# HGRN2 scan of a hybrid decoder: two of its mask levels computed by products of 64 keys and 32 queries

## The chip, the cores and the metric

The kernel runs on one core of a Trainium2 chip. The metric is the device time of one launch in microseconds, as the median over several runs. TensorE (PE in the profile) multiplies, VectorE (DVE) does elementwise work and reads the results, ScalarE (ACT) evaluates functions, GpSimd (POOL) splits weights into a high and a low part, and the SyncE queue (SP) loads the weights.

## The reference

Two decoder layers run on 512 prompt tokens and 8 groups of 4 sample tokens. Each layer is a half-step FFN, a mixer with three parallel recurrent branches (HGRN2, GLA, mLSTM) and a second half-step FFN. The change is in the first branch's scan, which computes:

```python
def gated_linear_scan(q, k, v, logf, s0):
    """S_t = diag(exp(logf_t)) S_{t-1} + k_t v_t^T ; o_t = S_t^T q_t, chunkwise and exactly per-token causal."""
    c = chunk_len(q.shape[2])
    tri = jnp.tril(jnp.ones((c, c), dtype=bool))

    def step(s, inp):
        qc, kc, vc, gc = inp
        b = jnp.cumsum(gc, axis=2)
        diff = b[:, :, :, None, :] - b[:, :, None, :, :]
        decay = jnp.exp(jnp.where(tri[:, :, None], diff, NEG_BIG))
        att = jnp.einsum('bhtd,bhsd,bhtsd->bhts', qc, kc, decay)
        o = (jnp.einsum('bhts,bhsv->bhtv', att, vc)
             + jnp.einsum('bhtd,bhdv->bhtv', qc * jnp.exp(b), s))
        ...
        return s_new, o
```

The scan has 4 heads with 128 features each. The matrix `att` holds, for a query t and a key s of one chunk, a product over the features in which each feature has a decay of its own.

## The kernel before

Activations lie with features on the 128 partitions and the 544 tokens along the free axis. Dense products (L723) run three times for each pair of operands: high by high, high by low, low by high. They take their weights from a stream that SP loads and POOL splits, and each is 128 x 128 weights by 272 tokens.

The kernel works on chunks of 128 tokens, so a head has four of them. The decay is a product over the tokens between key and query, so the kernel builds `att` in seven levels. Level l pairs blocks of 2^l tokens: the keys of a block's first half meet the queries of its second half. After each level, `qkt_update` multiplies decays into Q, K and T for the next level (L1949, L1952, L1956 on DVE), so that level l+1 can't be computed before level l has been read and updated.

A level is one step of the written-out order `ORDER`, of kind "lv". `weave` puts halves of dense tiles between the steps, one to four of them (`HALVES_BEHIND`), so that PE has work while DVE evaluates a step. PE's part of a step waits for `dve_step` and `act_step`, that is until both have done with the step before it. It increments `pe_step` with its last product. DVE's part waits for that and increments `dve_step` at its end (L2126).

In a level up to the fifth, PE computes for each head and chunk four products: 32 keys as the weights, by the 16 queries of these 32 tokens that lie in second halves (L915). The product of keys g to g+32 lands on partitions g to g+32 of PSUM tensor SA. That makes 4 x 4 x 4 = 64 products. Each product of 32-bit floats appears in the profile as two LDWEIGHTS and two MATMUL records, so a level has 128 MATMUL records. Levels 1 and 2 end with four products for the sample tokens (L835), eight records. The sixth and seventh level have one product for each block (L920): 32 keys by 32 queries, and 64 keys by 64 queries.

DVE reads SA with four COPY_PREDICATED instructions (L2015), one for each group of 32 partitions, under the level's mask of bytes. It writes only the 32 x 32 squares on the diagonal of `attC`.

The second branch (GLA, `br == 1`) uses the same code with two heads to a product. The scans follow one another in each of the two layers. In this profile the first branch's levels 1 to 7 begin on PE between 523 and 582 us in the first layer, and between 1924 and 1982 us in the second.

Of the kernel before, what the change touches and what calls it, by code (L numbers as in the profile page):

```python
# [32 lines left out]
HEADS, CH = 4, 128  # L33
NCH = SEQ // CH
# [205 lines left out]
def build(nc, wst, xT, par_d, lb_d, const_d, lvm_d, fg_d, st_h, st_g, st_c, st_n, st_m,  # L240
          yT, p_h, p_g, p_c, p_n, s_h, s_g, s_c, s_n, s_m, x_keep):
    ctx = ExitStack()
    with ctx:
# [110 lines left out]
        SA = ctx.enter_context(nc.psum_tensor("SA", [P, 2, 512], F32))  # L354
# [65 lines left out]
        half_of = const[:, C_DIAG + 100:C_DIAG + 102]  # L420
        pairs = const[0:SMP, C_DIAG + 104:C_DIAG + 108]
        colK = const[:, C_DIAG + 108:C_DIAG + 116]

        def mask(l):
            return lvm[:, (l - 1) * P:l * P]
# [7 lines left out]
        def kt(br, h):  # L433

            return h // 2 if br == 1 else h
# [271 lines left out]
        def _(pe):  # L707
# [153 lines left out]
            def step(L, s):  # L861
                kind, br, h = s
# [5 lines left out]
                mm = None  # L868
# [29 lines left out]
                elif kind == "d":  # L898
                    for i in range(2):
                        hh = 2 * h + i  # L900
# [4 lines left out]
                        mm = sample_products(br)  # L905
                elif kind == "lv":
                    bs, hf = 1 << h, 1 << (h - 1)
                    o = SA[:, 0, 0:HEADS * NCH * 16].rearrange("p (h c b) -> p h c b", h=HEADS, c=NCH)
                    n = 2 if br == 1 else 1
                    for hh in range(0, HEADS, n):  # L910
                        for c in range(NCH if hf < 32 else 0):
                            for g in range(4):
                                s0 = c * CH + 32 * g
                                q = Q[:, hh:hh + n, s0:s0 + 32].rearrange("p h (n b) -> p h n b", b=bs)[:, :, :, hf:bs]
                                mm = pe.matmul(o[32 * g:32 * g + 32, hh:hh + n, c, :].rearrange(  # L915
                                    "p h (n b) -> p h n b", b=hf), K[:, kt(br, hh), s0:s0 + 32], q, start=True, stop=True)
                        for c in range(NCH if hf >= 32 else 0):
                            for s0 in range(0, CH, bs):
                                o0 = c * 64 + s0 // bs * hf
                                mm = pe.matmul(SA[s0:s0 + hf, hh // 2, :].rearrange("p (h n) -> p h n", h=2)[  # L920
                                                   :, hh % 2:hh % 2 + n, o0:o0 + hf],
                                               K[:, kt(br, hh), c * CH + s0:c * CH + s0 + hf],
                                               Q[:, hh:hh + n, c * CH + s0 + hf:c * CH + s0 + bs],
                                               start=True, stop=True)
# [592 lines left out]
        def _(dve):  # L1517
# [446 lines left out]
            def step(L, s):  # L1964
# [40 lines left out]
                elif kind == "lv":  # L2005
                    dve.sem_inc(dve_began, 1)
                    bs, hf = 1 << h, 1 << (h - 1)
                    for s0 in range(0, CH if hf >= 32 else 0, bs):
                        n0 = s0 // bs * hf
                        a = attQ[s0:s0 + hf, :, :].rearrange("p h (c t) -> p h c t", t=CH)  # L2010
                        src = SA[s0:s0 + hf, :, :].rearrange("p a (b c t) -> p (a b) c t", b=2, c=NCH)
                        ch.did(dve.tensor_copy(a[:, :, :, s0 + hf:s0 + bs], src[:, :, :, n0:n0 + hf]))
                    for j in range(4 if hf < 32 else 0):
                        g = slice(32 * j, 32 * j + 32)
                        ch.did(dve.copy_predicated(  # L2015
                            attC[g, :, g].rearrange("p c (n b) -> p c n b", b=bs)[:, :, :, hf:bs],
                            mask(h)[g, g].rearrange("p (n b) -> p n b", b=bs)[:, :, hf:bs].unsqueeze(1).to_broadcast(
                                [32, HEADS * NCH, 32 // bs, hf]),
                            SA[g, 0, 0:HEADS * NCH * 16].rearrange("p (c n b) -> p c n b", c=HEADS * NCH, b=hf)))
                    if h <= S_LEVELS:  # L2020
                        ch.did(dve.copy_predicated(
                            attS,
# [328 lines left out]
```

## Time and profile before

| | |
|---|---|
| median of 3 runs | 2846.6 us (2843.3 to 2848.44) |
| the profiled execution | 2846.17 us, span 2844.4 us |
| PE busy | 2810.3 us, 99% of the span |
| DVE, ACT, POOL busy | 59%, 33%, 56% |
| TensorE clock granted, mean | 0.997 of full speed |
| share of PE in the chain that ended last | 93% |

A MATMUL record lasts longer than its place in the stream, since matmuls are pipelined. What a group of products costs PE is the distance from its first start to the start of the group behind it.

### The profile page before, as it was taken

What the parts mean: (1) busy time and instruction counts of PE and PEld (TensorE: products, weight loads), DVE (VectorE), ACT (ScalarE), POOL (GpSimd) and SP (SyncE); (2) the same over time, 40 slices, a digit from 0 to 9 for tenths busy, and PEclk for the clock granted to TensorE, in tenths of its full rate; (3) what the DMA queues carried; (4) which work ended last, traced back from release to release, by engine and by line L of the source; (5) the groups of instructions that cost most, each with busy time, mean ns of one, the idle gap of its engine ahead of it and who ended that gap; (6) DMA issues with size and microseconds to landing.
All of it is one profiled execution on the core that took longest, in us unless ns stands there. A gap on an engine that the chain in (4) does not pass through costs nothing.

```text
span 2844.4 us, 63198 instructions
## 1 busy us (share of the span) xinstructions
PE 2810.3 (99%) x24828; PEld 2766.3 (97%) x24828; DVE 1689.4 (59%) x2419; ACT 950.6 (33%) x1616; POOL 1596.5 (56%) x1466
## 2 busy tenths in 40 slices
PE   8999999999999999999999999999999999999998
PEld 7999999999999999999999999999999999999998
DVE  8554677545553578383784637766454446783645
ACT  4221233123152425151452414330412523452433
POOL 6666676556654674525464352766565556734343
PEclk9999999999999999999999999999999999999999
DMA  5796835665654655353444433355665557453532
GB/s 191 199 247 191 237 101 182 170 154 155 185 167 111 189 163 162 117 175 110 126 144 140 156 120 109 121 169 169 160 181 153 161 151 186 148 170 118 158 123 78
DMA packets 196956, 444.27 MB, mean 156 GB/s; under 512 B 13464, under 2 KB 57664, under 8 KB 195904
## 3 DMA queue, kind: packets, MB, share of 16 engines
q1 hardware_dynamic: 107360, 281.09, 30.4%
q0 software_dynamic: 40128, 125.83, 18.7%
q10 hardware_dynamic: 49248, 34.28, 4.0%
q8 instruction: 154, 2.52, 0.4%
q14 instruction: 66, 0.54, 0.1%
HBM read 422.64 MB, written 144.35 MB: 199 GB/s over the span
## 4 chain that ended last, share of the span: by engine, by line
PE 93%; DVE 3%; ACT 1%; POOL 1%; issue 1%; ACTq 0%; DVEq 0%; PEld 0%; POOLq 0%
PE dense L723 60%; PE SA L783 15%; PE SB L783 11%; POOL Wl L588 1%; PE SA L998 1%; PE SA L915 1%; PE SA L859 1%; PE SA L1001 1%; PE SA L903 1%; PE SA L846 0%; PE SA L920 0%; POOL Wh L586 0%; PE SB L1005 0%; PE SA L848 0%; PE SA L855 0%
## 5 line engine op out<-in xcount | busy, mean ns | idle before, releaser
L588 POOL TENSOR_TENSOR Wl<-raw,Wh 128x512 fp32r<-128x512 f32 x620 | 854.0, 1377 | 51.8
L586 POOL TENSOR_SCALAR Wh<-raw 128x512 fp32r<-128x512 f32 x620 | 450.9, 727 | 672.8 <-PEq L728 445.8
L723 PE MATMUL dense<-Hh,Wh 128*128 128x272 f32 x2768 | 585.8, 293 | 15.2 <-POOLq L590 10.1
L723 PE MATMUL dense<-Hh,Wl 128*128 128x272 f32 x2768 | 573.9, 289 | 0.5 <-issue 0.5
L723 PE MATMUL dense<-Hl,Wh 128*128 128x272 f32 x2768 | 572.6, 288 | 0.0
L723 PEld LDWEIGHTS dense<-Hh,Wh 128*128 128x128 f32 x2768 | 435.0, 189 | 25.7 <-issue 16.2
L723 PEld LDWEIGHTS dense<-Hl,Wh 128*128 128x128 f32 x2768 | 436.7, 189 | 0.0
L723 PEld LDWEIGHTS dense<-Hh,Wl 128*128 128x128 f32 x2768 | 434.0, 189 | 0.8 <-issue 0.8
L651 POOL TENSOR_TENSOR Sl<-pair,Sh 128x512 fp32r<-128x512 f32 x120 | 173.7, 1465 | 421.8 <-ACT Sh L1088 421.0
L723 PE MATMUL dense<-Ah,Wh 128*128 128x272 f32 x1408 | 291.9, 289 | 0.8 <-DVE X L1814 0.7
L723 PE MATMUL dense<-Al,Wh 128*128 128x272 f32 x1408 | 290.7, 288 | 0.0
L723 PE MATMUL dense<-Ah,Wl 128*128 128x272 f32 x1408 | 290.2, 287 | 0.0
L1814 DVE SCALAR_TENSOR_TENSOR X<-dense,X 128x544 f32 x64 | 46.3, 724 | 296.4 <-PE dense L723 295.9
L723 PEld LDWEIGHTS dense<-Ah,Wh 128*128 128x128 f32 x1408 | 220.6, 188 | 1.6 <-DVE X L1814 0.9
L723 PEld LDWEIGHTS dense<-Al,Wh 128*128 128x128 f32 x1408 | 221.3, 188 | 0.0
L723 PEld LDWEIGHTS dense<-Ah,Wl 128*128 128x128 f32 x1408 | 220.3, 189 | 0.0
L1088 ACT ACTIVATE Sh<-pair 128x512 fp32r<-128x512 f32 x240 | 143.9, 624 | 33.3 <-PE SA L783 33.2
L1088 ACT ACTIVATE Sh<-wsum 128x512 fp32r<-128x512 f32 x180 | 113.2, 630 | 100.0 <-PE SA L783 50.5
L1589 DVE TENSOR_TENSOR Sl<-wsum,Sh 128x512 fp32r<-128x512 f32 x180 | 136.3, 759 | 0.0
L1104 ACT ACTIVATE tmp<-SA 128x272 f32<-128x272 f32 x60 | 22.8, 381 | 269.1 <-PE SA L783 269.1
L1589 DVE TENSOR_TENSOR Sl<-pair,Sh 128x512 fp32r<-128x512 f32 x120 | 104.1, 867 | 12.4 <-ACT Sh L1088 12.4
L1681 DVE TENSOR_TENSOR Al<-tmp,Ah 128x544 f32 (+1 forms) x88 | 69.0, 784 | 40.9 <-ACT Ah L1130 20.9
(473 smaller groups left out, 6317.4 us busy)
## 6 DMA issues: line engine op xcount, KB each, us to landing
raw<-wst SPq DMA_DIRECT2D x276, 512.0 KB, 3.7
w_sums<-wst POOLq DMA_DIRECT2D x36, 1536.0 KB, 13.3
w_sums<-wst POOLq DMA_DIRECT2D x18, 2048.0 KB, 16.8
pair<-wst SPq DMA_DIRECT2D x120, 256.0 KB, 3.5
pair<-w_sums SPq DMA_DIRECT2D x60, 512.0 KB, 3.7
wsum<-w_sums SPq DMA_DIRECT2D x60, 512.0 KB, 3.6
w_sums<-w_sums POOLq DMA_DIRECT2D x12, 1536.0 KB, 9.0
wsum<-wst SPq DMA_DIRECT2D x60, 256.0 KB, 2.5
```

The source lines that it names most:

```text
L586: pool.tensor_scalar(Wh[:, j, cs], raw[:, j, cs], 1.0, 0.0, ALU.mult, ALU.add).then_inc(glink, 1)
L588: pool.tensor_tensor(Wl[:, j, cs], raw[:, j, cs], f32(Wh[:, j, cs]), ALU.subtract).then_inc(glink, 1)
L651: pool.tensor_tensor(Sl[:, q, :], slot(q), f32(Sh[:, q, :]), ALU.subtract).then_inc(q_lo_pool, 1)
L723: mm = pe.matmul(out[:, a, 0:HALF], w[:, ring, w0:w0 + 128], x[:, k, a * HALF:(a + 1) * HALF], start=(k == 0 and n == 0), stop=(k == nk - ...
L783: mm = pe.matmul(out, w[:, q, k * 128:(k + 1) * 128], xs[:, k, :], start=(opens and k == 0 and m == 0), stop=(k == 3 and m == 2), skip_gro ...
L859: return pe.transpose(out, in_, idn)
L903: mm = pe.matmul(SA[:, i, cs], K[:, kt(br, hh), cs], Q[:, hh, cs], start=True, stop=True)
L915: mm = pe.matmul(o[32 * g:32 * g + 32, hh:hh + n, c, :].rearrange("p h (n b) -> p h n b", b=hf), K[:, kt(br, hh), s0:s0 + 32], q, start=Tr ...
L1088: act.activation(Sh[:, q, :], slot(q), ACT.Copy).then_inc(q_hi, 1)
L1589: TT(Sl[:, q, :], slot(q), f32(Sh[:, q, :]), ALU.subtract).then_inc(q_lo, 1)
L1681: TT(Al[:, at, :], tmp[:, j:j + 1, :], f32(Ah[:, at, :]), ALU.subtract).then_inc(ffn_lo, 1)
L1814: STT(xs, dps[j % 2][:, :, 0:HALF], 0.5, xs, ALU.mult, ALU.add).then_inc(slot_free[j % 2], 1)
```

## The change

In the first branch alone, levels 2 and 4 take 64 keys and the 32 queries of these 64 tokens in one product. A level then has 4 x 4 x 2 = 32 products (64 MATMUL records) where it had 64 (128 records). A product lands on 64 partitions and 32 columns. Half of its result belongs to keys and queries of different groups of 32 and isn't read. The result of a level fills 512 columns of SA where it filled 256. DVE's four instructions stay in number, elements and destination. They read 16 columns out of each 32. Levels 1, 3, 5, 6 and 7, and the whole of the second branch, are as before.

```diff
--- before.py
+++ after.py
@@ -421,6 +421,10 @@
         pairs = const[0:SMP, C_DIAG + 104:C_DIAG + 108]
         colK = const[:, C_DIAG + 108:C_DIAG + 116]
 
+        def level_keys(br, l):
+
+            return 64 if br == 0 and l in (2, 4) else 32
+
         def mask(l):
             return lvm[:, (l - 1) * P:l * P]
 
@@ -905,15 +909,16 @@
                         mm = sample_products(br)
                 elif kind == "lv":
                     bs, hf = 1 << h, 1 << (h - 1)
-                    o = SA[:, 0, 0:HEADS * NCH * 16].rearrange("p (h c b) -> p h c b", h=HEADS, c=NCH)
+                    wide = level_keys(br, h)
+                    o = SA[:, 0, 0:HEADS * NCH * wide // 2].rearrange("p (h c b) -> p h c b", h=HEADS, c=NCH)
                     n = 2 if br == 1 else 1
                     for hh in range(0, HEADS, n):
                         for c in range(NCH if hf < 32 else 0):
-                            for g in range(4):
-                                s0 = c * CH + 32 * g
-                                q = Q[:, hh:hh + n, s0:s0 + 32].rearrange("p h (n b) -> p h n b", b=bs)[:, :, :, hf:bs]
-                                mm = pe.matmul(o[32 * g:32 * g + 32, hh:hh + n, c, :].rearrange(
-                                    "p h (n b) -> p h n b", b=hf), K[:, kt(br, hh), s0:s0 + 32], q, start=True, stop=True)
+                            for g in range(0, CH, wide):
+                                s0 = c * CH + g
+                                q = Q[:, hh:hh + n, s0:s0 + wide].rearrange("p h (n b) -> p h n b", b=bs)[:, :, :, hf:bs]
+                                mm = pe.matmul(o[g:g + wide, hh:hh + n, c, :].rearrange(
+                                    "p h (n b) -> p h n b", b=hf), K[:, kt(br, hh), s0:s0 + wide], q, start=True, stop=True)
                         for c in range(NCH if hf >= 32 else 0):
                             for s0 in range(0, CH, bs):
                                 o0 = c * 64 + s0 // bs * hf
@@ -2010,13 +2015,15 @@
                         a = attQ[s0:s0 + hf, :, :].rearrange("p h (c t) -> p h c t", t=CH)
                         src = SA[s0:s0 + hf, :, :].rearrange("p a (b c t) -> p (a b) c t", b=2, c=NCH)
                         ch.did(dve.tensor_copy(a[:, :, :, s0 + hf:s0 + bs], src[:, :, :, n0:n0 + hf]))
+                    wide = level_keys(br, h)
                     for j in range(4 if hf < 32 else 0):
                         g = slice(32 * j, 32 * j + 32)
                         ch.did(dve.copy_predicated(
                             attC[g, :, g].rearrange("p c (n b) -> p c n b", b=bs)[:, :, :, hf:bs],
                             mask(h)[g, g].rearrange("p (n b) -> p n b", b=bs)[:, :, hf:bs].unsqueeze(1).to_broadcast(
                                 [32, HEADS * NCH, 32 // bs, hf]),
-                            SA[g, 0, 0:HEADS * NCH * 16].rearrange("p (c n b) -> p c n b", c=HEADS * NCH, b=hf)))
+                            SA[g, 0, 0:HEADS * NCH * wide // 2].rearrange("p (c e t) -> p c e t", c=HEADS * NCH, t=16)[
+                                :, :, j % (wide // 32), :].rearrange("p c (n b) -> p c n b", b=hf)))
                     if h <= S_LEVELS:
                         ch.did(dve.copy_predicated(
                             attS,
```

## Rows read from the trace of the kernel before

**Rows 1.** The page, engine busy times, clock by slices and chain that ended last

```profile
PE 2810.3 (99%) x24828; PEld 2766.3 (97%) x24828; DVE 1689.4 (59%) x2419; ACT 950.6 (33%) x1616; POOL 1596.5 (56%) x1466
...
PE 93%; DVE 3%; ACT 1%; POOL 1%; issue 1%; ACTq 0%; DVEq 0%; PEld 0%; POOLq 0%
```

**Rows 2.** Waits of PE over the span: who waited for whom, total us, times, longest

```profile
PE SA L915 <- issue: 2.2, 2, 1.7
PE SA L915 <- DVEq L2126: 1.4, 4, 0.5
```

**Rows 3.** Timeline of PE, level 1, first layer: start, us, record, idle before

```profile
523.25 1.24 PE L915 MATMUL SA<-setA,kbuf 128*32 128x16 f32 x126
...
524.36 0.39 PE L835 MATMUL SB<-setA,kbuf 128*32 128x32 f32 x7
524.67 0.52 PE L723 MATMUL dense<-Hh,Wh 128*128 128x272 f32 x2
```

**Rows 4.** Timeline of PE, level 4, first layer

```profile
555.86 1.26 PE L915 MATMUL SA<-setA,kbuf 128*32 128x16 f32 x128 [0.50 <-DVEq L2126]
557.05 0.52 PE L723 MATMUL dense<-Hh,Wh 128*128 128x272 f32 x2
```

**Rows 5.** Timeline of PE, levels 6 and 7, first layer

```profile
574.04 1.21 PE L920 MATMUL SA<-setA,kbuf 128*32 128x32 f32 x64
575.18 0.40 PE L723 MATMUL dense<-Hh,Wh 128*128 128x272 f32 x1
...
581.40 2.08 PE L920 MATMUL SA<-setA,kbuf 128*64 128x64 f32 x32
583.41 0.40 PE L723 MATMUL dense<-Hh,Wh 128*128 128x272 f32 x1
```

**Rows 6.** Timeline of PE, third branch, second layer: products of 64 weight columns

```profile
2297.38 0.63 PE L965 MATMUL SA<-ones,kbuf 128*64 128x1 f32 x16
2297.87 0.38 PE L970 MATMUL SA<-const,kst 128*64 128x4 f32 x8
2298.10 0.61 PE L965 MATMUL SA<-ones,kbuf 128*64 128x1 f32 x16
...
2299.97 0.38 PE L970 MATMUL SA<-const,kst 128*64 128x4 f32 x8
2300.28 0.52 PE L723 MATMUL dense<-ohB,Wh 128*128 128x272 f32 x2
```

**Rows 7.** Timeline of PE, diagonal products, first layer, two calls

```profile
507.00 1.95 PE L903 MATMUL SA<-setA,kbuf 128*128 128x128 f32 x16
508.88 0.44 PE L835 MATMUL SB<-setA,kbuf 128*32 128x32 f32 x8
...
512.36 1.95 PE L903 MATMUL SA<-setA,kbuf 128*128 128x128 f32 x16
514.06 0.50 PE L723 MATMUL dense<-Hh,Wh 128*128 128x272 f32 x2
```

**Rows 8.** Timeline of PE, level 2, first layer

```profile
533.88 1.10 PE L915 MATMUL SA<-setA,kbuf 128*32 128x16 f32 x109
536.65 0.33 PE L915 MATMUL SA<-setA,kbuf 128*32 128x16 f32 x18 [1.66 <-issue]
```

**Rows 9.** Timeline of PE, level 2, second layer

```profile
1935.94 0.94 PE L915 MATMUL SA<-setA,kbuf 128*32 128x16 f32 x88
1937.40 0.49 PE L915 MATMUL SA<-setA,kbuf 128*32 128x16 f32 x37 [0.53 <-issue]
```

**Rows 10.** Timeline of DVE, levels 2 and 4, first layer

```profile
537.40 2.99 DVE L2015 COPY_PREDICATED att<-lvm,SA 32x256 f32<-32x256 uint8 x4 [4.41 <-PE SB L835]
...
557.32 1.88 DVE L2015 COPY_PREDICATED att<-lvm,SA 32x256 f32<-32x256 uint8 x4 [0.53 <-PE SA L915]
```

**Rows 11.** Busy time, PE's granted clock and DMA by stretches of the span

```profile
537.90:541.40 3.50, 3.50 (x18) 3.50 (x17) 3.38 (x6) 0.00 (x0) 0.00 (x0) 0.51 1.04 389
...
899.80:906.60 6.80, 6.80 (x46) 6.78 (x45) 4.50 (x13) 0.00 (x0) 3.78 (x4) 0.50 1.10 194
```

## The prediction

> **What bounds the kernel now.** I read the page first. PE is busy for 2810.3 of 2844.4 us and holds 93% of the chain that ended last, while no other engine is above 59% [rows 1]. So the time is the length of PE's stream, and a microsecond added to it or taken from it anywhere is a microsecond of the span, unless PE was waiting there. Next I read the waits of PE: in the changed line, L915, it waited 2.2 us for nothing that the profile shows ("issue") and 1.4 us for the end of DVE's step before [rows 2]. These are the only places where an edit of L915 could be hidden or could give something back. The timeline of PE around the levels gives the prices.
>
> **The measure.** The work of the two changed levels is small: four steps in all (levels 2 and 4, in two layers). A level in the old form without disturbance costs PE 1.19 us for 128 records from its first start to the start of the dense product behind it [rows 4], 9.3 ns a record. Level 1, with the sample products behind it, takes 1.42 us from 523.25 to 524.67, of which the last seven sample records hold 0.31 and the 128 records 1.1 [rows 3]. Level 2 has the same shape, so that is its undisturbed price too.
>
> **What a product of 64 keys and 32 queries costs.** The trace of before has no such product, so I bound it by the rows around it, per MATMUL record.
> - By level 6: 32 keys by 32 queries, on two separate groups of PSUM partitions, 64 records in 1.14 us, 17.7 ns each [rows 5]. This is the new form but for the number of weight columns. With 16 queries and four groups of partitions a record costs 9.3, so a group of partitions gets one every 37 ns (4 x 9.3) there and every 35 ns (2 x 17.7) in level 6: twice the queries, the same interval. So the queries don't set it at 16, and what is left is the load of 32 weight columns.
> - By the third branch: 64 weight columns by one or four columns of data, alternating between two groups of 64 partitions, 24 records in the 0.72 us from 2297.38 to 2298.10 [rows 6]. Without the first ones it is 8 records in 0.23, 29 ns each, or one every 58 ns in a group. That is with next to no data to stream, so it is the load of 64 columns: nearly twice the interval of 32.
> - By level 7: 64 keys by 64 queries, all on the same 64 partitions, 32 records in 2.01 us, 62.8 ns each [rows 5]. If loading and multiplying came one behind the other within a group, this record would take at least 58 + 35 = 93 ns. So a load runs beside the product before it, and the longer of the two sets the pace.
>
> The new form has the load of 64 columns (58 ns in a group) and the stream of 32 queries (at most 35 ns). I take the longer one, with both groups of partitions side by side: 29.2 ns a record, 64 records in 1.87 us. The lower end is the price by level 6, 17.7 ns (1.14 us), or even 9.3 ns (0.60 us) if only the count of records mattered. The upper end is level 7's 62.8 ns (4.0 us), if the two groups did not run side by side. Row 6 is nearest, since it shares the weights' shape and the alternation, and it differs only in the side that is not the longer one.
>
> The page "TensorE: Matmul & The Clock Gate" of the Trainium skill, section "LDWEIGHTS (loading the stationary operand)", says that a load's time goes with its columns alone, columns / 1.2 ns, which makes 26.7 and 53.3 ns here. By that rule a level would go from 128 / 4 x 26.7 = 0.85 us to 64 / 2 x 53.3 = 1.71 us, and the four steps would cost 3.4 us more. The rows above give nearly the same intervals (35 to 37 and 58 ns), with some nanoseconds on top, so by that rule, too, the change lengthens PE's stream although it halves its records.
>
> **The sum for PE.** Level 4: 1.87, plus the 0.08 us by which the eight records ahead of a dense product took longer in row 6 (0.31 against 0.23), is 1.95 against 1.19: +0.76. Level 2: 1.87 + 0.31 for the sample products, and a change of shape from 64 to 32 columns between them that the old form did not have. Nearest for that is the pair of diagonal steps, 1.88 us when 32-column products follow and 1.70 when dense ones do: 0.17 [rows 7]. So 2.35 against 1.42: +0.93. In two layers this is 2 x (0.76 + 0.93) = +3.4 us.
>
> **Is it hidden?** No. At level 4 PE waits 0.50 us for DVE before the step [rows 4] and at level 5 again (part of the 1.4 us of [rows 2]), but the first wait is over when the step starts. DVE's part of level 4 starts when PE's part ends, and so does the dense work that PE does meanwhile. A later end shifts both alike, and the wait at level 5 stays.
>
> **DVE.** Four reads of 256 elements stay four reads of 256 elements with the same destination. They took 2.99 us in level 2 and 1.88 in level 4 [rows 10]; that difference comes with the same source layout, so it is the runs of 2 and 8 elements in the destination and the mask, which stay. The source now comes in runs of 16 instead of one. I price it at nothing. The bound below is nothing as well, as no element goes. The bound above is level 4 at level 2's price: 1.1 us, in two layers 2.2, and this would fall in full on PE, which already waits for DVE at level 5. In level 2 it would be hidden by the slack that DVE has (it sat idle for 4.4 us before it [rows 10]).
>
> **The stalls inside level 2.** In the first layer PE stops for 1.66 us behind 109 of 128 records, in the second 0.53 us behind 88, both times with nothing that it waited for [rows 8, 9]. The old form takes a weight load and a matmul every 9 ns or so, faster than any other part of PE's stream. So I read these stalls as the supply of instructions running dry: it lasts 218 instructions in one case and 176 in the other. The new step 2 has 128 such instructions and takes longer over them, so neither place exists any more, and behind it comes dense work that takes few instructions a microsecond. I expect 2.2 us back. From 537.9 to 541.4, right behind the longer stall, PE's granted clock is 0.51 (the 1.2 GHz level), and there PE lost about 3.5 x 0.49 = 1.7 us [rows 11]. PE had stood still and done small products before it fell. Without the stall I expect no fall: 1.7 us back.
>
> **Total.** 3.4 - 2.2 - 1.7 = -0.5 us. The profiled execution took 2846.17 us (span 2844.4 and 1.8 around it), so the same execution would take 2845.7. The median of the runs shown is 0.4 above it. I predict 2846 us: no change that a measurement of this kernel can tell, for which I take 0.2% or 5.7 us. What is removed and what is added are each smaller than that.
>
> **Rivals.**
> - *The stalls stay, or move to a neighbour.* The instructions that level 2 no longer has shift all that follows, and level 3 still has its 256. A stall there with a fall of the clock would cost what the old one did. Against it: levels 1 and 4 of the first layer show none [rows 3, 4], so most steps go without. Then the sum is +3.4, 2849.6 us: still within 0.2%.
> - *The number of products decides.* If a record cost 9.3 ns whatever its shape, each step would take 0.60 us, 0.6 less, and the four steps 2.4 less; with the stalls gone 2840 us, just faster. Against it stand rows 5 and 6, where records cost 17.7, 29 and 63 ns. The same page, section "Back-to-back issue gap", gives every matmul of up to 64 columns about 60 cycles, which would favour the change; row 4's 9.3 ns shows that no such floor holds between different groups of partitions here.
> - *The other side, slower: the two halves of PE's columns don't work at once.* At level 7's 62.8 ns a step costs 4.0 us, 2.8 more (2.9 plus the change of shape in level 2); in four steps 11.8, less 3.9 for the stalls: 2854 us. It turns slower than 0.2% from (5.7 + 3.9) / 4 = 2.4 us a step more, or about 55 ns a record. Row 6 speaks against it.
> - *The clock falls in the longer thin steps.* In the first layer 2.9 us of row 6's form came just ahead of a stretch of 6.8 us at 0.50 [rows 11], a loss of 3.4; in the second layer they did not. A new step of 1.9 us, behind a wait of 0.5 at level 4, is shorter and streams 32 columns, so I think it holds the clock. Two such falls would give 3.4 - 2.2 - 1.7 + 6.8 = +6.3 us, 2852.5; one leaves the time within 0.2%.
> - *DVE's reads get dearer*: +2.2 us on the forecast, 2848.
>
> **How the numbers follow.** The forecast has 0.60, the stalls that stay or move 0.27, the count of products 0.04, halves one after the other 0.03, the clock 0.04, DVE 0.02. Faster is the count of products alone, 0.04. Slower are the two that end at 2852.5 and 2854, 0.07. All the rest, 0.89, is within 0.2%. The range must hold the first two with the spread that the runs before have, 3 us to either side of the median: 2842 reaches 4 below the forecast, 2852 takes in the stalls that stay with 2 us on top. This leaves out the count of products and the two slow rivals.
>
> **What would show it.** In the profile after, 64 records of 128x32 on 128*64 in each of four steps, with 1.87 us from the first to the sample products in level 2 and 1.95 to the dense product in level 4. 17.7 ns a record would show that the load doesn't set the pace, 63 that the halves take turns. In level 2 no idle "issue" before L915 and no clock of 0.5 behind it; the reads of L2015 at 2.99 and 1.88 us; the wait for L2126 before level 5 at 0.3. The prediction is wrong if the price of a record is off by more than 20 ns, or if PE's clock falls in more than one of the new steps.

## The result, and the profile after

The changed kernel takes 2850.96 us (median of 19 runs, 2847.83 to 2856.29) against 2846.6 us (19 runs, 2843.3 to 2853.73). The ratio is 1.0016, with a 95% interval of 1.0009 to 1.0023: 4.6 us slower, between 2.6 and 6.5. The forecast was 2846, half a microsecond faster. The time lies in the range that was given, but the direction is the other one, and the interval excludes no change.

The profiled execution has a span of 2847.6 us, 3.2 more than before. The timeline of PE (start, us, record, count, idle before it) shows the changed steps of level 2, in the first and the second layer, and of level 4, in the first:

```profile
533.71 2.06 PE L920 MATMUL SA<-setA,kbuf 128*64 128x32 f32 x64
535.70 0.44 PE L839 MATMUL SB<-setA,kbuf 128*32 128x32 f32 x8
536.07 0.52 PE L727 MATMUL dense<-Hh,Wh 128*128 128x272 f32 x2
...
1933.80 2.06 PE L920 MATMUL SA<-setA,kbuf 128*64 128x32 f32 x64
1935.79 0.44 PE L839 MATMUL SB<-setA,kbuf 128*32 128x32 f32 x8
1936.16 0.52 PE L727 MATMUL dense<-Hh,Wh 128*128 128x272 f32 x2
...
554.76 2.06 PE L920 MATMUL SA<-setA,kbuf 128*64 128x32 f32 x64 [0.52 <-DVEq L2133]
556.75 0.52 PE L727 MATMUL dense<-Hh,Wh 128*128 128x272 f32 x2
```

A step of 64 records now takes 1.99 us (533.71 to 535.70, 554.76 to 556.75), 31.1 ns a record. With the sample products level 2 takes 2.36 us from its first start to the dense product, against 1.42 undisturbed [rows 3]: +0.94. Level 4 takes 1.99 against 1.19 [rows 4]: +0.80. In two layers that is +3.5 us. The pauses inside level 2 [rows 8, 9] are gone.

The same timeline shows two pauses that the kernel before did not have, inside level 3 of the first layer and in the dense work behind level 5 of the second:

```profile
545.27 0.95 PE L920 MATMUL SA<-setA,kbuf 128*32 128x16 f32 x91
547.54 0.51 PE L920 MATMUL SA<-setA,kbuf 128*32 128x16 f32 x37 [1.31 <-issue]
...
1967.83 0.29 PE L727 MATMUL dense<-Hh,Wl 128*128 128x272 f32 x1
1970.89 0.60 PE L727 MATMUL dense<-Hh,Wl 128*128 128x272 f32 x1 [2.77 <-issue]
```

PE's waits over the whole span, as in [rows 2]:

```profile
PE dense L727 <- issue: 3.3, 2, 2.8
...
PE SA L920 <- DVEq L2133: 1.9, 4, 1.0
PE SA L920 <- issue: 1.3, 1, 1.3
```

Without a releaser PE now waits 4.6 us. Before it was 3.2: the 2.2 of [rows 2], and 1.0 in dense work, two pauses of about half a microsecond in the second layer. The spell at half clock behind level 2 [rows 11] is gone, but one stands behind the pause at 1968 us (the busy time by stretch; the third column from the right is the granted clock):

```profile
1970.80:1974.20 3.40, 3.31 (x14) 3.31 (x15) 0.00 (x0) 0.00 (x0) 0.00 (x0) 0.50 0.43 145
```

DVE's reads (the timeline of DVE, levels 2 and 4 of the first layer; before in [rows 10]) cost what they did:

```profile
536.31 3.02 DVE L2021 COPY_PREDICATED att<-lvm,SA 32x256 f32<-32x256 uint8 x4 [3.50 <-PE SB L839]
...
557.00 1.85 DVE L2021 COPY_PREDICATED att<-lvm,SA 32x256 f32<-32x256 uint8 x4 [1.33 <-PE SA L920]
```

The gains that I had set against the longer steps did not come: +3.5 us for the steps, and +1.4 where the forecast had -2.2 for the pauses. A small third term is the wait for DVE's steps, which went from 1.4 to 1.9 us. Level 4 of the second layer waits 1.0 us where it waited 0.4, and the pause of 0.4 us behind level 3 ahead of it is gone. That the one follows from the other is not shown.

These terms are more than the 3.2 us by which the profile's span grew. Against them stand other small waits (0.8 us less) and the clock. Over the whole span, but for its end, PE stood at half clock for 13.7 us before and for 10.2 after, which is 1.7 us less time: the spell at 899.8 us [rows 11] is gone as well, and one at 1841.1 us is new. The second profile of the changed kernel has only 6.8 us of it. The runs show no such gain: their mean granted clock is 0.996 in both kernels.

The experiments ask two things: what sets the price of a step, and what decides where PE pauses.

### The profile page after: what moved, and what is told of

It is laid out like the page before. It is cut to its first block, busy times and chain, and to the rows that moved or that the text cites. A ratio compares the mean times of both kernels' runs of the same rounds, so it can differ in the third digit from the quotient of the medians.

```text
span 2847.6 us, 62686 instructions
## 1 busy us (share of the span) xinstructions
PE 2812.5 (99%) x24572; PEld 2768.9 (97%) x24572; DVE 1687.7 (59%) x2419; ACT 950.8 (33%) x1616; POOL 1599.0 (56%) x1466
## 4 chain that ended last, share of the span: by engine, by line
PE 93%; DVE 3%; ACT 1%; POOL 1%; issue 1%; ACTq 0%; DVEq 0%; PEld 0%; POOLq 0%
PE dense L727 60%; PE SA L787 15%; PE SB L787 11%; POOL Wl L592 1%; PE SA L920 1%; PE SA L1003 1%; PE SA L863 1%; PE SA L1006 1%; PE SA L907 1%; PE SA L850 0%; PE SA L925 0%; POOL Wh L590 0%; PE SB L1010 0%; PE SA L852 0%; DVE kbuf L1957 0%
## 5 line engine op out<-in xcount | busy, mean ns | idle before, releaser
L727 PE MATMUL dense<-Hh,Wh 128*128 128x272 f32 x2768 | 586.3, 293 | 13.9 <-POOLq L594 10.0
```

The source lines that it names most:

```text
L727: mm = pe.matmul(out[:, a, 0:HALF], w[:, ring, w0:w0 + 128], x[:, k, a * HALF:(a + 1) * HALF], start=(k == 0 and n == 0), stop=(k == nk - ...
```

## The experiments

All times are medians, and ratios are to the kernel before on the same chip, with 95% intervals. Each chip has its own median of the kernel before, 2846.2 to 2847.8 us. "Pauses" is the sum of PE's waits without a releaser in one profiled execution. Some of these executions are not typical: those of e4_twice and e8_before_moved are the longest of their runs (2864.6 and 2875.1 us), and that of f128_after took 2860.8.

| run | us | ratio | pauses, us |
|---|---|---|---|
| before, and profiled again | 2846.6 | | 3.2, 4.0 |
| changed, and profiled again | 2851.0 | 1.0016 | 4.6, 6.6 |
| e1_level2 | 2851.1 | 1.0015 (1.0007 to 1.0024) | 4.2 |
| e2_level4 | 2853.1 | 1.0033 (1.0018 to 1.0049) | 8.2 |
| e3_half | 2842.7 | 0.9986 (0.9977 to 0.9995) | 2.3 |
| e4_twice | 2859.2 | 1.0041 (1.0026 to 1.0055) | 7.6 |
| e5_load | 2851.7 | 1.0016 (1.0007 to 1.0024) | 3.2 |
| e6_phase | 2857.6 | 1.0038 (1.0026 to 1.0050) | 9.3 |
| f64_before | 2851.9 | 1.0020 (1.0011 to 1.0029) | 6.9 |
| f128_before | 2853.6 | 1.0022 (1.0012 to 1.0033) | 6.2 |
| f192_before | 2855.3 | 1.0033 (1.0020 to 1.0046) | 8.7 |
| f256_before | 2849.9 | 1.0014 (1.0004 to 1.0023) | 4.1 |
| f128_after | 2854.6 | 1.0025 (1.0014 to 1.0036) | 12.0 |
| e7_after_moved | 2866.5 | 1.0057 (1.0040 to 1.0075) | 6.7 |
| e8_before_moved | 2866.4 | 1.0056 (1.0038 to 1.0073) | 12.8 |
| e9_phase_moved | 2875.8 | 1.0090 (1.0073 to 1.0107) | 12.1 |
| e10_level4_moved | 2869.8 | 1.0076 (1.0056 to 1.0095) | 6.3 |

**What sets the price of a step**

*e5_load.* Products of 64 keys and only 16 queries, with half of the results of these levels left out:

```diff
-  q = Q[:, hh:hh + n, s0:s0 + wide].rearrange("p h (n b) -> p h n b", b=bs)[:, :, :, hf:bs]
-  mm = pe.matmul(o[g:g + wide, hh:hh + n, c, :].rearrange(
+  q = Q[:, hh:hh + n, s0:s0 + 32].rearrange("p h (n b) -> p h n b", b=bs)[:, :, :, hf:bs]
+  mm = pe.matmul(o[g:g + wide, hh:hh + n, c, 0:16].rearrange(
```

> Levels 2 and 4 by products of 64 keys and only 16 queries (those of the first 32 tokens of the 64; the other half is left out). The load theory expects the price of a record to stay at 31 ns and a step at 1.99 us, since it is the 64 weight columns that set the pace, so the same time as with the change. The rival, that queries and weights add up or that the 32 queries set the pace, expects 18 to 25 ns a record, 1.2 to 1.6 us a step, and 1.5 to 3 us less than with the change.

The timeline of PE, level 4 of the first layer:

```profile
553.76 2.04 PE L920 MATMUL SA<-setA,kbuf 128*64 128x16 f32 x64 [1.00 <-DVEq L2133]
555.74 0.52 PE L727 MATMUL dense<-Hh,Wh 128*128 128x272 f32 x2
```

With half the queries a step takes 1.98 us (553.76 to 555.74), against 1.99. So the queries add nothing. The 64 weight columns set the pace, with two groups of partitions in place of four. The stream has the changed kernel's instructions in number and order, and the pause behind level 5 of the second layer is there (2.77 us). The one inside level 3 of the first is not.

*e3_half.* The old form with half of its products, that is, with two of four chunks of each head left out of levels 2 and 4:

```diff
-  for c in range(NCH if hf < 32 else 0):
+  for c in range(NCH // 2 if br == 0 and h in (2, 4) else NCH if hf < 32 else 0):
```

> As the kernel before, but levels 2 and 4 of the first scan compute only the first two chunks of each head: 32 products of 32 keys and 16 queries, so half of these two levels is left out. PE's stream has the same instructions in the same order and number as with the change, only the shape of 128 records a layer differs. The load theory expects 0.6 us a step, 0.6 less than before: 2.4 us less than before in all, and 5.9 us less than with the change. The supply theory expects the pauses where the profile after has them (inside level 3 of the first layer, behind level 5 of the second), not where before has them. If the number of products set the price of a step, it would cost what the change's steps cost, 2.0 us.

The timeline of PE, level 4 and level 3 of the first layer:

```profile
552.64 0.73 PE L915 MATMUL SA<-setA,kbuf 128*32 128x16 f32 x64 [0.52 <-DVEq L2126]
553.33 0.49 PE L723 MATMUL dense<-Hh,Wh 128*128 128x272 f32 x2
...
543.60 0.95 PE L915 MATMUL SA<-setA,kbuf 128*32 128x16 f32 x91
545.42 0.51 PE L915 MATMUL SA<-setA,kbuf 128*32 128x16 f32 x37 [0.86 <-issue]
```

With the changed kernel's number of instructions but the old shape, a step takes 0.69 us. So the count does not set the price either: the same number of records costs 0.69 us with 32 weight columns and 1.99 with 64. This kernel is 8.3 us faster than the changed one, of which 5.2 are the four steps (4 x 1.3). Of the two places that were expected for the pauses one is right to the record: it comes again with 37 records of level 3 to go, as in the profile after. The second, behind level 5 of the second layer, did not come. So that one, the longest of the changed kernel, does not come from the shorter stream alone.

*e4_twice.* The changed form with each product done twice, so that the number of instructions is the old one:

```diff
-  for g in range(0, CH, wide):
+  for g in [g for g in range(0, CH, wide) for _ in range(wide // 32)]:
```

> Each product of 64 keys and 32 queries in levels 2 and 4 is done twice in a row, into the same place. So the stream has exactly the kernel before's number of instructions, in the changed shape. The load theory expects 128 records at 31 ns, 4.0 us a step, 2.8 us more than before: +11.2 us in four steps. On the pauses inside level 2: if they came from taking instructions too fast for their supply, they are gone here, since the step takes 31 ns a record in place of 9; if they come from the place in the stream alone, they are inside level 2 again, 0.5 to 1.7 us.

The undisturbed steps, of the second layer, take 3.87 us each for 128 records, 30 ns a record where 31 were expected. The step of level 2 in the first layer takes 4.07, with no pause, where the old shape had 1.7. A pause of 2.75 us came inside level 4 of the first layer instead, with 22 records to go, and one of 4.5 us behind level 5 of the second. So taking instructions slowly clears a place, but it doesn't keep PE from pausing elsewhere. The time came out at 11.7 us more by the ratio.

**One level at a time**

*e1_level2* and *e2_level4* differ from the changed kernel in one line:

```diff
-            return 64 if br == 0 and l in (2, 4) else 32
+            return 64 if br == 0 and l == 2 else 32    # e1_level2
+            return 64 if br == 0 and l == 4 else 32    # e2_level4
```

> Only level 2 is computed by products of 64 keys and 32 queries. The load theory (a group of 64 partitions gets a product's half each time 64 weight columns are loaded, 31 ns a record as in the profile after) expects 1.99 us for the 64 records and 2.36 us with the sample products, against 1.42 undisturbed: +0.94 us in each layer, +1.9 us in all. The supply theory (PE's pauses without a releaser lie where the instruction stream crosses certain places, so they move with the number of instructions ahead) expects level 3's pause of the first layer after, 1.3 us, since the stream up to there is the same, and other places behind it. Together 2847 to 2850 us. The rival, that the whole loss comes from level 4 (where DVE is late), expects no more than +0.5 us.

> Only level 4 is computed by products of 64 keys and 32 queries. The load theory expects 1.99 us for the step against 1.19: +0.8 us in each layer, +1.6 in all. The supply theory expects the pauses inside level 2 to be there as in the kernel before (1.7 us in the first layer, 0.5 in the second), since the stream up to there is unchanged. Together about +1.6 us. The rival, that the loss is DVE's reads with gaps, expects L2021 at level 4 above 1.88 us and a longer wait before level 5.

The steps were as expected (1.99 us each), the times were not: +4.3 and +6.2 us by the medians, where the steps are worth +1.9 and +1.6. By the ratios it is 4.3 (2.0 to 6.8) and 9.4 (5.1 to 13.9). DVE's read at level 4 of e2_level4 takes 1.86 us, so the rival that it gets dearer is out. In e1_level2 there is a pause of 4.2 us inside level 5 of the first layer, and not the one inside level 3 that I had named. Its profile also has 20.5 us at half clock against 13.7, which costs 3.4 us. In e2_level4 the pause inside level 2 of the first layer is as before. The one in the second layer is gone: I had expected it, but the stream up to there is shorter by the first layer's level 4. One of 1.4 us in level 3 of the second layer and one of 4.75 behind its level 5 are new. The timeline of PE at the longest pause of e1_level2 and of e2_level4:

```profile
567.84 0.31 PE L920 MATMUL SA<-setA,kbuf 128*32 128x16 f32 x8 [4.20 <-issue]
...
1973.96 0.39 PE L727 MATMUL dense<-Hh,Wl 128*128 128x272 f32 x1 [4.75 <-issue]
```

The two halves of the change together cost less than the sum of the two alone. That they cost less than level 4 by itself, as the medians have it, is within the intervals. In e2_level4 most of the lost time is not the steps' price, and the rival of e1_level2 (that level 4 alone loses) is out.

**Is a pause where it is by chance?**

*before_again* and *after_again* are the two kernels, profiled once more.

> The kernel before, profiled once more. If the pauses without a releaser belong to places in the instruction stream, they are inside level 2 in both layers and behind level 3 of the second again; if they come from the traffic of the moment, they are elsewhere or of other lengths. The spells of half clock are expected to differ.

> The changed kernel, profiled once more. By the place in the stream: pauses inside level 3 of the first layer (1.3 us) and behind level 5 of the second (2.8 us) again. By the traffic of the moment: elsewhere. The steps of levels 2 and 4 are expected at 1.99 us again.

The timeline of PE in before_again and then in after_again:

```profile
533.85 1.10 PE L915 MATMUL SA<-setA,kbuf 128*32 128x16 f32 x109
536.89 0.33 PE L915 MATMUL SA<-setA,kbuf 128*32 128x16 f32 x18 [1.94 <-issue]
```

```profile
545.17 0.95 PE L920 MATMUL SA<-setA,kbuf 128*32 128x16 f32 x91
547.70 0.51 PE L920 MATMUL SA<-setA,kbuf 128*32 128x16 f32 x37 [1.58 <-issue]
```

The pauses come behind the same record, 109 of 128 in one kernel and 91 in the other, and are some 0.3 us longer than in the first profiles. All the others of the first scan are at their places too, and after_again has one more. The half clock behind level 2 came again in before_again. So these pauses belong to the program.

**What moves a pause**

*e6_phase.* The kernel before, with half of level 1's products done twice. Nothing is shorter or in another order; all behind is 128 instructions later in PE's stream, and 256 in the second layer, since each layer has the extra products.

```diff
-  for g in range(4):
+  for g in [*range(4)] + [*range(2)] * (br == 0 and h == 1):
```

> The kernel before with 32 of the 64 products of level 1 of the first scan done twice, so that all behind it comes 128 instructions later in the stream. The extra records cost 64 x 9.3 ns = 0.6 us a layer, 1.2 us in all. The supply theory expects the pauses to leave the places that they have before (inside level 2 in both layers) for others, with a time between 1 us less and 5 us more than before. If they don't hang on the place in the stream, they stay inside level 2, and the time is 1.2 us more.

It takes 11 us more than the kernel before, where the extra records account for 1.2 and 5 was the most that I expected. The pauses grew from 3.2 to 9.3 us, and level 2 of the first layer has none. The profile, whose span is 11.7 us longer, also has 23.9 us at half clock against 13.7, which costs another 5. By itself this kills the idea on which my forecast rested, that a pause is a matter of the step in which it stands.

*f64_before to f256_before.* The clean form of the same test: 16, 32, 48 or 64 small products that nobody reads, ahead of all levels in each layer. In the first layer they shift the levels by 64 to 256 instructions, as the names say, and in the second by twice that.

```diff
                 elif kind == "d":
+                    for g in [x % 4 for x in range(16 if (br, h) == (0, 1) else 0)]:
+                        pe.matmul(SB[32 * g:32 * g + 32, 1, 0:16], K[:, 0, 32 * g:32 * g + 32],
+                                  Q[:, 0, 0:16], start=True, stop=True)
```

> The kernel before with 16 small products more (32 keys by 16 queries, into a bank that nobody reads) at the start of the second diagonal step of the first scan: everything behind it comes 64 instructions later in PE's stream, at a cost of 16 x 2 x 9.3 ns = 0.3 us a layer. The place theory expects the pauses without a releaser to leave the places of the kernel before, and a time between 1 us less and 8 us more than the 0.6 us of the products. If the place in the stream had nothing to do with it, the pauses stay inside level 2 and the time is 0.6 us more.

> The same with 32 small products, a shift by 128 instructions, 0.6 us a layer. The place theory expects the pauses of the run that doubled half of level 1, which shifted the later levels as far: about 4 us inside level 5 of the first layer and 1 us inside level 2 of the second, and a time of 5 to 11 us more than before. Without the place: 1.2 us more.

> The same with 48 small products, a shift by 192 instructions, 0.9 us a layer. The place theory expects pauses at other places than with 64 or 128. Without the place: 1.8 us more.

> The same with 64 small products, a shift by 256 instructions, 1.2 us a layer. If PE's instructions come in blocks of 256 (an estimate from transfers of 16 KB), this shift brings the blocks' edges back to the same instructions, and the pauses are those of the kernel before: 1.7 and 0.5 us inside level 2, 0.4 us behind level 3 of the second layer. The time is then 2.4 us more than before. By traffic or by the amount shifted: no return.

The timeline of PE at the pauses, in f256_before (level 2, first and second layer) and then in f128_before (level 1 and level 5 of the first layer, level 2 of the second):

```profile
537.55 0.33 PE L918 MATMUL SA<-setA,kbuf 128*32 128x16 f32 x18 [1.66 <-issue]
...
1940.96 0.49 PE L918 MATMUL SA<-setA,kbuf 128*32 128x16 f32 x37 [2.05 <-issue]
```

```profile
527.55 0.18 PE L918 MATMUL SA<-setA,kbuf 128*32 128x16 f32 x1 [1.30 <-issue]
568.84 0.26 PE L918 MATMUL SA<-setA,kbuf 128*32 128x16 f32 x8 [3.65 <-issue]
...
1942.96 0.49 PE L918 MATMUL SA<-setA,kbuf 128*32 128x16 f32 x37 [0.80 <-issue]
```

Shifted by 256 instructions (512 in the second layer), the first scan has its pauses inside level 2 again, with 18 and 37 records to go, exactly as in [rows 8, 9]; that of the first layer is of the same 1.66 us, and that of the second is longer. Two small ones of the second layer did not return, and a new one of 0.4 us stands ahead of the levels. Shifted by 128, the one in level 2 of the first layer is gone, and one of 3.65 us stands in level 5, with 8 records to go. In e6_phase it is also in level 5, with 8 to go and 3.65 us long. Shifted by 64 and 192, the first layer has its pauses in other places again (with 49 records of level 2 and 5 of level 3 to go in f64_before, 69 of level 3 in f192_before). The whole curve is 2846.9 (the kernel before on this chip), 2851.9, 2853.6, 2855.3 and 2849.9 us for shifts of 0 to 256, of which the added products are 0, 0.6, 1.2, 1.8 and 2.4. Net of them the four shifted ones are at +4.4, +5.5, +6.6 and +0.7 us by the medians, and at 5.1, 5.1, 7.6 and 1.6 by the ratios, give or take some 3 us. So a change of nothing but the place in the stream costs 4 to 8 us, more than the 3.5 us of the change's shape. The kernel before happens to stand at the best of the four places.

The second layer says the same, since its shifts are twice as large. The pause of level 2 with 37 records to go came again in the three kernels here whose shift there is 256 or 512 (e6_phase, f128_before, f256_before). With 128 and 384, which again differ by 256, f64_before and f192_before both have one at one and the same dense product:

```profile
1960.61 0.61 PE L723 MATMUL dense<-Hl,Wh 128*128 128x272 f32 x2 [2.17 <-issue]
...
1965.70 0.41 PE L723 MATMUL dense<-Hl,Wh 128*128 128x272 f32 x2 [2.14 <-issue]
```

In all the traces it is one rule. I numbered everything that a trace has of PE's two queues (weight loads, matmuls and what their sequencer records) in order of time, and took the number of the record behind each pause modulo 256. The 19 profiles have 59 pauses that end with a transfer of instructions (the eight others are in the last part of this section). In the first layer it is 79 or 80 for all 28, and in the second 225 or 226 for all 31. So the pauses stand 256 records apart, or a multiple of that, whether the step is quick, slow (e4_twice, level 4) or dense. But not every such place has one: level 3 pauses in the changed kernel and in e3_half, and not in e1_level2 and e5_load, with the same stream up to there. What decides between them is open.

*f128_after.* The same shift of 128 on the changed kernel.

> The changed kernel with 32 small products more in the second diagonal step, a shift of all levels by 128 instructions, 0.6 us a layer. By the place in blocks of 256: level 3 stands where it stands in the kernel before, so the pause of 1.3 us inside it in the first layer goes; level 5 stands where it stands in the kernel before shifted by 128, so it gets that one's pause of 3.6 us in the first layer. The time by the sum of these: the changed kernel's plus 1.2 for the products plus 2 to 4, 2853 to 2857 us. If the change's remaining loss did not hang on the place: 2852 us.

The timeline of PE in the first layer of f128_after, level 1 and level 5:

```profile
526.32 0.18 PE L923 MATMUL SA<-setA,kbuf 128*32 128x16 f32 x1 [1.30 <-issue]
...
564.39 1.19 PE L923 MATMUL SA<-setA,kbuf 128*32 128x16 f32 x120 [0.16 <-DVEq L2136]
573.61 0.30 PE L923 MATMUL SA<-setA,kbuf 128*32 128x16 f32 x8 [8.03 <-issue]
```

Both halves of the expectation came: level 3 has no pause (it takes 1.20 us, as before), and level 5 has one with 8 records to go, as in f128_before. That it is 8.03 us long in place of 3.65 was not expected. PE's clock fell to 0.50 at 569.0 us, 3.4 us into this pause, and stayed there for 10.2 us, of which 5.6 lie behind the pause (the columns are those of the stretches above):

```profile
565.50:569.00 3.50, 0.08 (x8) 0.00 (x0) 0.15 (x1) 0.00 (x0) 0.00 (x0) 1.00 1.19 427
569.00:573.60 4.60, 0.00 (x0) 0.00 (x0) 0.00 (x0) 0.00 (x0) 0.00 (x0) 0.50 0.31 132
573.60:579.20 5.60, 5.59 (x31) 5.55 (x31) 4.92 (x7) 0.00 (x0) 4.83 (x4) 0.50 0.01 3
```

The shift takes the changed kernel to 2854.6, as expected, and the profiled execution is 6 us above that, so a pause of 8.03 us is not shown for the others.

**What sets a pause's length**

Each of the 59 pauses ends 2.2 to 2.9 us after the start of a 16 KB transfer of the instruction queue (q8 in the list of DMA queues: kind, packets, MB, share). In the profile after one starts between 545.25 and 545.35, and PE goes on at 547.54. In the kernel before one starts between 534.25 and 534.35, and PE goes on at 536.65 [rows 8]. In f128_after, PE stands still from 565.5 on. The queues' list for 565.5 to 571.1, and then for 571.1 to 571.3:

```profile
q0 software_dynamic: 32, 2.03, 96.1%
q1 hardware_dynamic: 19, 0.05, 2.4%
```

```profile
q8 instruction: 1, 0.02, 27.7%
q0 software_dynamic: 1, 0.00, 0.3%
```

For 5.6 us POOL's queue had all 16 DMA engines at 96% with 32 large packets (a copy from `w_sums` to `w_sums`), and no instruction packet was moved. Then one was, and PE went on 2.4 us later. That made me expect that without this traffic long pauses become short, and I moved the 24 transfers into `w_sums` away from the first scan:

```diff
-SUMS_AT = tuple(range(8, 80, 3))
+SUMS_AT = (*range(1, 14, 3), *range(28, 83, 3))
```

> The changed kernel, with POOL's 24 large transfers into w_sums of each mixer placed at other pieces of the weight stream, none of them while the first scan's levels run. The traffic theory (a block of PE's instructions comes some 2.3 us after its transfer starts, and that transfer starts late when a w_sums transfer has the DMA engines full, so that a pause of a microsecond becomes one of 3 to 5) expects the pause of 2.8 us behind level 5 of the second layer to shrink to below 1.7 us or go, with no half clock behind it: 1 to 4 us less than the changed kernel, 2847 to 2850 us. The rival, that a pause's length hangs on the place in the stream alone, expects the same pauses in the same places and 2851 us.

> The kernel before with the same move of the w_sums transfers. Its pauses (1.7 us and 0.5 us inside level 2, 0.5 and 0.4 elsewhere in the second layer) end 2.3 us after the start of their instruction transfer, so none of them is lengthened much by traffic. The traffic theory expects the pauses to stay and the time to change by less than 2 us from the kernel before. If the pauses went altogether, the traffic would be their cause and not only what lengthens them.

> The kernel before with 32 products of level 1 done twice (128 instructions more in the stream of each layer), and the w_sums transfers moved away. Without the move this took 11 us more than the kernel before, with pauses of 4.5, 3.6 and 1.2 us in the level steps. The traffic theory expects the pauses of 4.5 and 3.6 us to shrink to 1.7 us or less each and the half clock behind them to go, so 5 to 9 us less: 2848 to 2852 us. By the place alone: 2857 us again.

> Only level 4 changed, and the w_sums transfers moved away. Without the move its second layer had a pause of 4.8 us behind level 5 with half clock behind it, and pauses of 1.9 and 1.5 us inside level steps. The traffic theory expects the one of 4.8 us to shrink to 1.7 us or less, and the other two to stay: 3 to 5 us less than without the move, 2848 to 2850 us. By the place alone: 2853 us again.

The times don't answer, since the new places cost 15 to 19 us elsewhere in all four. Of that, 4.7 to 6.7 us are two standstills in dense work, at 1020 to 1033 and at 2428 to 2442 us, which the table counts as pauses. They are of another kind: no other run has them, no transfer of the instruction queue comes in them or in the 4 us before, and they stay at the same dense product whatever the shift. Of the first scan's pauses, some do answer. The second layer's scan has none in any of the four, and the first layer's has none in e7 either. In e7 and e10 the long ones behind level 5 of the second layer (2.8 and 4.8 us) are gone, and in e9 that of level 1 shrank from 4.5 to 1.8 us at the same record. But in e9 that of level 5 stayed at 3.65 us, with 8 records to go and no packet of POOL's queue near, and e8 got one of 5.1 us where the kernel before had none. The timeline of PE in e9_phase_moved, level 1 and level 5 of the first layer:

```profile
531.02 0.18 PE L915 MATMUL SA<-setA,kbuf 128*32 128x16 f32 x1 [1.82 <-issue]
573.78 0.31 PE L915 MATMUL SA<-setA,kbuf 128*32 128x16 f32 x8 [3.65 <-issue]
```

So with POOL's traffic gone some pauses shrink or go, but one of 3.65 us comes without it, and the theory as I had put it falls. The changed kernel and the kernel before took the same time here (2866.5 and 2866.4). Their profiles have 0 and 7.1 us of the first kind of pause, but that of e8 is of its longest run, so how the steps' 3.5 us were made up for is not shown.

## Why the prediction was wrong, step by step

- **What bounds the kernel: right.** PE's stream sets the time, and what was added to it appeared in the span. Next to nothing took up the longer steps: the wait before level 5 is 0.1 us shorter in each layer, and what I had said of that wait, that it stays, was off by this much.
- **The price of a product: right, a little low.** 31.1 ns a record against 29.2 forecast (0.23 us for eight records, as its row has it, would be 28.8). e5_load shows that it goes with the 64 weight columns and not with the queries, and e3_half that it is not the number of products. Row 6, the load without data to stream, was the right neighbour.
- **The sum for PE: right.** +3.5 us against +3.4; level 2 +0.94 (0.93), level 4 +0.80 (0.76).
- **DVE at nothing: right.** 3.02 and 1.85 us, against 2.99 and 1.88.
- **"I expect 2.2 us back": this step failed.** It was right that the pauses inside level 2 go. It was wrong that nothing would come in their place. I had read them as what the step itself did, by taking instructions fast, and so as something that leaves with the step. They stand at certain places of the instruction stream, to the record, in both profiles of each kernel. The change takes 128 instructions out of each of the two steps, and so moves levels 3 and 4 of the first layer by 128, the later ones by 256, and the second layer by 256 more. PE's pauses went from 3.2 us to 4.6, in the second profiles from 4.0 to 6.6: +1.4 to +2.6 in place of -2.2. The place is not all of it. The pause behind level 5 of the second layer, 2.8 of the 4.6 us, is at the same record in every kernel that has level 4 in the new form and POOL's transfers where they were (both profiles of the changed kernel, e2_level4, e4_twice, e5_load, f128_after). It is in none with the old form, though e3_half, the kernel before, f128_before and f256_before stand at the same place there. So it came with the new form of level 4, and how is open.
- **"Without the stall I expect no fall: 1.7 us back": it failed with it.** The fall behind level 2 went, and one of the same 3.4 us came behind the new pause in the second layer. In the second profile that pause was longer (3.27 us) and the clock did not fall. So a fall can't be booked to one pause, in either direction.
- **The rival "the stalls stay, or move to a neighbour"** was the case, with the place that it named, level 3, and 2849.6 us against 2851.0 measured. It had 0.27. Its argument against, that most steps show no pause, was no argument: what counts is whether one of the places falls on the step, and a shift by 128 instructions picks a new set of them. The shifts of the kernel before show that the old set was a good one: the three others cost 4 to 8 us.

The price of the shape is shown, and so is that pauses stand only at places 256 records apart in the stream. That some of the 4.6 us is pauses is shown by the profiles; how much of it in the mean of many runs is not, since the steps account for 3.5 and the interval reaches from 2.6 to 6.5. Open is why the transfer of a block starts late even without POOL's traffic (3.65 us in e9_phase_moved), what decides which of the places pauses, why the new form of level 4 brings one behind level 5 of the second layer, and where the moved transfers lost most of their 15 to 19 us.

## What to carry to other kernels

Halving the number of small matmuls by widening their weights does not pay where the load of the weight columns sets the pace: count columns loaded per group of partitions, not products alone. Where many small matmuls follow one another in a long unrolled stream, count also the instructions: a pause without a releaser stood only at places 256 records apart, and an edit that adds or removes instructions moves these places for all that follows. So don't book such a pause as a gain because the step in which it stood is changed. Before an effect of a few microseconds is believed, shift the stream by some harmless instructions (here in four steps up to 256) and see how far the time moves by that alone.

## What the runs showed of the hardware

- The pauses of PE that end with a 16 KB transfer of the instruction queue (59 in 19 profiles, 0.2 to 8.0 us) end 2.2 to 2.9 us after its start. They all stand at one number modulo 256 of PE's records in a layer. In a second profile of the same program they came at the same records, with one more in the changed kernel. With the DMA engines filled at 96% by large packets of another queue, the transfer began only when they had ebbed, and the pause was 8.03 us long. Without such packets one of 3.65 us came as well.
- A shift of the stream by 64, 128 or 192 instructions alone made the kernel 4 to 8 us slower, net of the instructions' own time; 256 brought the main pauses back to their records.
- In one and the same form (32 weight columns, 16 queries) a record costs 9.3 ns, in another (64 columns, 16 or 32 queries) 31 ns, whatever the queries.
- After a standstill of 2.8 us PE's clock was at 0.50 for 3.4 us, and after one of 3.3 us at the same record of the same kernel it did not fall. In one of 8.0 us it fell 3.4 us after the start and stayed at 0.50 for 10.2 us.
